# Differential attention: scores from fp32r halves, the next maximum ahead of the subtraction, scores two steps ahead, and local attention in the same order

## The reference

```
s_lat = einsum('bkgqd,bksd->bkgqs', qb, kb) * scale       # |k_pos - q_pos| <= 128
s_ctx = einsum('bkgqd,bkcd->bkgqc', qb, k_ctx) * scale
p = softmax(concatenate([sink_col, s_lat, s_ctx]))
```

```
s = einsum("bqmd,bkmd->bmqk", q_blk * 32 ** -0.5, kf)      # m: 2 maps x 6 heads
p = softmax(s - slopes[:, None, None] * |qpos - kpos|)
a = p[:, :, 0] - lam * p[:, :, 1]
o = einsum("bhqk,bkhe->bqhe", a, vf)
```

## Time and profile before

| | |
|---|---|
| time, median of 3 runs | 4617.31 us (4612.63 to 4624.49) |
| the profiled execution's own time | 4616.67 us |
| its span, first to last instruction | 4614.9 us |
| mean granted TensorE clock | 0.94 |
| TensorE busy (matmul) | 4279.6 us, 93% |
| VectorE, ScalarE, GpSimd busy | 2053.8, 1427.2, 324.4 us |
| differential attention, first layer, first score to last output | 2898.05 to 3025.46 us |
| the same, second layer | 3996.82 to 4126.30 us |
| local attention's steps | about 509 to 653 us |

### The profile page before, as it was taken

How to read it: one execution, slowest core, us unless ns; L and a number is a source line. 1 busy time by engine, 2 the same in 40 slices (tenths; PEclk the granted TensorE clock), 3 DMA queues, 4 the chain that set the end, 5 groups by cost and what they waited for, 6 DMA issues and landing times. The chain is left out here.

```text
span 4614.9 us, 50711 instructions
## 1 busy us (share of the span) xinstructions
PE 4279.6 (93%) x21093; PEld 3224.0 (70%) x21093; DVE 2053.8 (45%) x3082; ACT 1427.2 (31%) x2094; POOL 324.4 (7%) x320
## 2 busy tenths in 40 slices
PE   7899879999999999899999799989998979998998
PEld 2288457788888777578878478457786658546876
DVE  0131566312365333362373564553474455364366
ACT  0121453211253121242361222333462132142254
POOL 0000012000000000000000242000000223100000
PEclk9999888999999999899999899889999989789999
DMA  7611001111112111122222000022222100002231
GB/s 253 236 62 36 9 6 37 55 64 64 56 63 74 55 62 62 38 91 92 97 85 87 6 1 1 5 64 83 91 91 75 40 6 1 5 28 64 91 100 64
DMA packets 254387, 288.69 MB, mean 63 GB/s; under 512 B 6436, under 2 KB 226619, under 8 KB 254197
## 3 DMA queue, kind: packets, MB, share of 16 engines
q1 hardware_dynamic: 254197, 286.04, 18.6%
HBM read 283.92 MB, written 2.10 MB: 62 GB/s over the span
## 5 line engine op out<-in xcount | busy, mean ns | idle before, releaser
L443 PE MATMUL banks<-h_halves,w_halves 128*128 128x512 f32 x3824 | 1426.0, 373 | 84.0 <-DVE h_halves L256 42.4
L444 PE MATMUL banks<-h_halves,w_halves 128*128 128x512 f32 x3824 | 1422.0, 372 | 0.0
L445 PE MATMUL banks<-h_halves,w_halves 128*128 128x512 f32 x3824 | 1414.9, 370 | 0.0
L443 PEld LDWEIGHTS banks<-h_halves,w_halves 128*128 128x128 f32 x3824 | 729.4, 191 | 223.2 <-issue 74.4
L445 PEld LDWEIGHTS banks<-h_halves,w_halves 128*128 128x128 f32 x3824 | 727.1, 190 | 126.0
L444 PEld LDWEIGHTS banks<-h_halves,w_halves 128*128 128x128 f32 x3824 | 729.3, 191 | 119.9
L256 DVE TENSOR_TENSOR w_halves<-work,w_halves 128x2048 fp32r<-128x2048 f32 (+1 forms) x215 | 488.3, 2271 | 549.4 <-ACT w_halves L251 549.3
L251 ACT ACTIVATE w_halves<-work 128x2048 fp32r<-128x2048 f32 (+1 forms) x215 | 407.1, 1894 | 563.2 <-PE banks L445 429.6
L251 ACT ACTIVATE h_halves<-kept 128x512 fp32r<-128x512 f32 (+1 forms) x520 | 332.4, 666 | 314.0 <-PE banks L445 235.2
L256 DVE TENSOR_TENSOR h_halves<-kept,h_halves 128x512 fp32r<-128x512 f32 (+1 forms) x520 | 361.2, 736 | 138.8 <-ACT h_halves L251 138.1
L846 PE MATMUL banks<-work,kept 128*2 128x512 f32 x384 | 170.1, 597 | 10.3 <-DMA work<-in_mod_w 10.3
(11 more groups left out here) (351 smaller groups left out, 4937.2 us busy)
## 6 DMA issues: line engine op xcount, KB each, us to landing
work<-in_w_ff SPq DMA_DIRECT2D x64, 1024.0 KB, 5.1
work<-in_mod_w SPq DMA_DIRECT2D x24, 2048.0 KB, 7.9
work<-in_ffn_w_in SPq DMA_DIRECT2D x44, 1024.0 KB, 5.1
work<-in_odd_w_in SPq DMA_DIRECT2D x24, 1024.0 KB, 5.2
work<-in_w_in SPq DMA_DIRECT2D x24, 1024.0 KB, 4.9
work<-in_ffn_w_out SPq DMA_DIRECT2D x16, 1024.0 KB, 4.9
work<-in_even_w_in SPq DMA_DIRECT2D x13, 1024.0 KB, 5.1
work<-in_odd_w_out SPq DMA_DIRECT2D x8, 1024.0 KB, 4.8
```

Of the source, the lines that this page charges most:

```text
L443: nc.tensor.matmul(o, low[:, k - a, fc], rh[:, tc], start=(k == 0), stop=False)
L444: nc.tensor.matmul(o, high[:, k - a, fc], rl[:, tc], start=False, stop=False)
L445: mm = nc.tensor.matmul(o, high[:, k - a, fc], rh[:, tc], start=False, stop=(k == K - 1))
```

## The change

In differential attention q and k are split into high and low parts, once a stage, three tiles of 128 features each. The scores of a step become the two bias matmuls, then three passes (low q by high k, high q by low k, high by high) of two fp32r matmuls each: the first of a pass is that of map 0 into its bank, the second that of map 1, on the next 32 rows, into the other. The scaling of q moves from GpSimd into the split. The first tile is split ahead of the steps, the second and third in steps 1 and 5. TensorE issues `scores(s+2)` where it issued `scores(s+1)`, and VectorE runs `top(s+1)` ahead of `subtract(s)`. The order of local attention is changed in these two places too, with nothing else in it changed.

```diff
@@ window_stage
             scores(0)
+            scores(1)
             for s in range(N):
-                if s + 1 < N:
-                    scores(s + 1)
+                if s + 2 < N:
+                    scores(s + 2)
                 if s:
                     weigh(s - 1)
                 turn(s)
...
             for s in range(N):
-                normalise(s)
                 if s + 1 < N:
                     top(s + 1)
+                normalise(s)
                 if s:
                     out(s - 1)
@@ diff_stage
+    part = lambda n: core.w_halves[:, n * SEQ:(n + 1) * SEQ]
+    high = [[part(6 * n + t) for t in range(3)] for n in range(2)]
+    low = [[part(6 * n + 3 + t) for t in range(3)] for n in range(2)]
+    tiles_of = lambda n, t: u2(core, 4 + 3 * n + t)
...
+    split_at = {1: 1, 5: 2}
...
         def _(pool):
-            for t in range(3):
-                nc.gpsimd.tensor_scalar(u2(core, 4 + t), u2(core, 4 + t), scale, None, ALU.mult).then_inc(q_scaled, 1)
             pool.wait_ge(loads_in, 80)
-            nc.gpsimd.tensor_copy(dist16, dist).then_inc(q_scaled, 1)
+            nc.gpsimd.tensor_copy(dist16, dist).then_inc(dist_made, 1)
...
                 if s >= 2:
                     pe.wait_ge(exped, 2 * (s - 1))
                 pe.wait_ge(slope_made, h + 1)
+                banks = [core.ps[:, (s % 2) * 2 + m, :] for m in range(2)]
                 for m in range(2):
-                    mp = 2 * h + m
-                    pp = slice((mp % 4) * DD, (mp % 4 + 1) * DD)
-                    bank = core.ps[:, (s % 2) * 2 + m, :]
-                    nc.tensor.matmul(bank, si[h % 2], dist16[:, 3 * P - i * P:3 * P - i * P + SEQ], start=True, stop=False)
-                    mm = nc.tensor.matmul(bank, u2(core, 4 + mp // 4)[pp, i * P:(i + 1) * P],
-                                          u2(core, 7 + mp // 4)[pp, :], start=False, stop=True)
+                    nc.tensor.matmul(banks[m], si[h % 2], dist16[:, 3 * P - i * P:3 * P - i * P + SEQ], start=True,
+                                     stop=False)
+                pe.wait_ge(low_done, 2 * (h // 2) + 2)
+                for n, (q, k) in enumerate(((low[0], high[1]), (high[0], low[1]), (high[0], high[1]))):
+                    for m in range(2):
+                        mp = 2 * h + m
+                        pp = slice((mp % 4) * DD, (mp % 4 + 1) * DD)
+                        mm = nc.tensor.matmul(banks[m], q[mp // 4][pp, i * P:(i + 1) * P], k[mp // 4][pp, :], start=False,
+                                              stop=(n == 2))
                 mm.then_inc(scored, 1)
...
+            def split(t):
+                for n in range(2):
+                    nc.scalar.activation(high[n][t], tiles_of(n, t), ACT.Copy, scale=(scale, 1.0)[n]).then_inc(high_done, 1)
+
+            split(0)
             act.wait_ge(lam_s, 1)
...
             for s in range(N):
                 if s + 1 < N:
                     exps(s + 1)
+                if s in split_at:
+                    split(split_at[s])
                 copy(s)
...
+            def split(t):
+                for n in range(2):
+                    dve.wait_ge(high_done, 2 * t + n + 1)
+                    nc.vector.scalar_tensor_tensor(out=low[n][t], in0=tiles_of(n, t), scalar=(scale, 1.0)[n],
+                                                   in1=high[n][t].bitcast(F32), op0=ALU.mult,
+                                                   op1=ALU.subtract).then_inc(low_done, 1)
+
+            split(0)
             dve.wait_ge(v_turned, 1)
...
             for s in range(N):
-                subtract(s)
                 if s + 1 < N:
                     top(s + 1)
+                subtract(s)
+                if s in split_at:
+                    split(split_at[s])
                 if s:
                     out(s - 1)
```

More of the change, by code:

```diff
@@ L2347, in diff_stage @@
     sc = lambda s, c, w=2: core.sb(GX0 + (s % 2) * 8 + c, w)
+    part = lambda n: core.w_halves[:, n * SEQ:(n + 1) * SEQ]
+    high = [[part(6 * n + t) for t in range(3)] for n in range(2)]
+    low = [[part(6 * n + 3 + t) for t in range(3)] for n in range(2)]
+    tiles_of = lambda n, t: u2(core, 4 + 3 * n + t)
     steps = [(h, i) for h in range(6) for i in range(4)]
     N = len(steps)
-    (loads_in, lam_s, v_turned, v_copied, slope_made, q_scaled, scored, maxed, exped, subtracted, turned,
-     turned_copied, weighted, out_done, chain_s) = core.sems(15)
+    split_at = {1: 1, 5: 2}
+    (loads_in, lam_s, v_turned, v_copied, slope_made, dist_made, high_done, low_done, scored, maxed, exped, subtracted, turned,
+     turned_copied, weighted, out_done, chain_s) = core.sems(17)
     with nc.Block() as block:
@@ L2376, in _ @@
             mm.then_inc(v_turned, 1)
-            pe.wait_ge(q_scaled, 4)
+            pe.wait_ge(dist_made, 1)
             def scores(s):
```

## The result

The changed kernel took 4533.02 us (median of 4 runs, 4532.26 to 4538.15), beside 4616.16 us for the kernel before in the same session (4612.63 to 4624.49). The ratio is 0.9824 [0.9807, 0.984]. The saving is 83 us; 4545 (4520 to 4585) was forecast, a saving of 72. The profiled execution took 4533.55 us, with a span of 4531.8 and a mean granted clock of 0.944.

What follows compares the result with a forecast made beforehand. Differential attention was taken as bound by TensorE at the lower clock level, by a 4.51 us engine ring close to TensorE's 4.25 at the upper; 4616.7 - 31 - 33 - 8 = 4545 us, range 4520 to 4585.

Steps and rivals of the forecast that it cites:

- The ring and the bound: Differential attention, upper level: engine loop of 4.51 us close to TensorE's 4.25; new step 3.35 us, VectorE the bound.
- The pairs run together: Differential attention's scores: each pass's two matmuls overlap, six taking 0.68 us at the upper level and 1.3 at the lower.
- Time at the lower level: Each differential attention stage: 25 us at the lower clock level (1.2 GHz), between an immediate rise and the old 36.
- The first intervals: Start of each differential attention stage: steps of 5.1 us at the lower clock level, TensorE the bound.
- The splits: Splitting q and k in differential attention: 1 us charged a stage; step 5's hidden or up to 1.5 us of VectorE.
- The sum for layer 1, between the maxima: Layer 1's differential attention: 4.4 steps at 5.1 us, 18.6 at 3.35 = 62.3, 1 for splits; whole stage 96 us.
- Local attention: Local attention: the new order removes a wait, saving 8 us of at most 9.4 us of TensorE idle.
- B: Differential attention's score pairs run one after the other, upper step 3.43 us, 107 us a stage: 4565 us; chance 0.15.
- E: The reordering does nothing, upper step stays 4.51 us, local attention gives 0: 4599 us; chance 0.02.
- C: Differential attention: TensorE stands at scores(s+2) while weigh and turn could go, upper step 4.0 us: 4569 us; chance 0.12.
- D: Differential attention: the clock level rises at once, 86 us a stage, savings 41 and 43: 4525 us; chance 0.11.
- A: Clock stays at the lower level through both differential attention stages: 4609 us, or 4673 without pair overlap; chance 0.06.

Runs made afterwards that it cites:

- experiment 1: The changed kernel with the old orders put back in both attentions, so the scores from halves alone: 4591.67 us, ratio 0.9957 to the kernel before.
- experiment 2: The kernel before with both stages' new orders and its f32 scores kept, no splits: 4599.9 us, ratio 0.9965 to the kernel before.
- experiment 4: The changed kernel with both maps' scores multiplied from the same 32 rows, those of map 0: 4568.3 us, ratio 0.9895 to the kernel before.
- experiment 10: The changed kernel with all splits ahead of the steps and differential attention's output copy on ScalarE: 4519.33 us; with two filling matmuls added, 4521.15 us.
- experiment 3: The changed kernel, in differential attention only: maximum behind the subtraction again, 4595.64 us; or instead scores one step ahead again, 4672.14 us.

## Why the prediction was right

The mechanism was right in the steps that carry the saving (two close limits, pairs that run together, VectorE as the new bound), and the size was 11 us short: 6.7 and 4.9 us in the two layers and 2.3 outside the stages, less 2.8 in local attention. Part of the nearness is luck, since terms of both signs were off. By its own steps:

- **The ring and the bound.** Right. "Shortening one alone would stop at the other" is what experiments 1 and 2 measured: 4.51 and 4.24 us a step. VectorE is the new bound; its step is 3.22 or less, not 3.35. Negation and reciprocal now stand together and start 0.08 apart (2957.72, 2957.80), where the 1.46 for maximum and negation had charged 0.20 from the negation's start on.
- **The pairs run together.** Right, and shown by experiment 4, which took the cause away. The size was not 0.68 us for six but 0.89, and at the lower level 1.58, not 1.3. The price of one matmul was right: inside the group the starts are 0.23 and 0.43 us apart, as in the earlier trace rows. What the sum left out are the group's two ends, where TensorE goes from 128 rows to 32 and back: 0.33 and 0.32 instead of 0.23, and 0.59 and 0.56 instead of 0.43. With the same ends six one at a time take 1.58 us, not 1.36, so the rivals without overlap were priced too low as well. The estimate by the Trainium skill's ratio (TensorE: Matmul & The Clock Gate, Part 3) was 0.89 and 1.7 us. The first agrees with the measurement by chance: it charges 0.30 us a pair, and the distance inside the group is 0.23. The extra 0.2 us cost little at the upper level, since TensorE's 2.93 stays at or under VectorE's step.
- **Time at the lower level.** 21.8 and 26.5 us, forecast 25. The number was near by luck, and the shape was not: one stretch of 15 or 16 us, and a second that the split in step 5 brought about and the prediction didn't have.
- **The first intervals.** Charged 5.1 us each; they were 2.5, 3.1 and 5.6. The first two are short since the scores of steps 0 to 2 issue before any weigh or turn; the third has VectorE's wait at `out` in it (experiment 10). Worth 4.1 us a stage.
- **The splits.** Here the cost was larger than forecast. I charged 1 us a stage, at most 1.5 of VectorE. The split in step 1 cost nothing. That in step 5 cost 1.9 (5.1 beside 3.2), and the lower level behind it more: maxima fell by 4.0 and 4.3 us without it.
- **The sum for layer 1, between the maxima.** Forecast 4.4 x 5.1 + 62.3 + 1 = 85.7 us, measured 79.0. The first three intervals gave 4.1 us less, the fourth 1.5 (3.6 for 5.1), the fifth 1.1 (3.0 for 4.05), fifteen upper ones at 3.14 gave 3.2, and the split's interval and the two of the dip behind it (5.1, 5.2, 3.9) took back 3.1: together 6.7, but for rounding.
- **Local attention.** Forecast 8 us, got 5.2. Of the 9.4 us of idle in the earlier trace rows about 1.7 lay in the last steps behind 645 us, which no order fills, and 3.9 stay between 529.2 and 645. All of that is TensorE's weigh waiting for ScalarE's copy (3.9 us, 16 waits); the same wait was 7.2 us in 20 before, from 527 to 645. The stage's start also stayed at the lower level 20.3 us instead of 17.8, which the prediction didn't have; what part of the missing 2.8 us that makes was not separated. TensorE is busy 97% at the upper level, not over 98.

The rivals: B is refuted by experiment 4. E, by which the reordering does nothing, is refuted by experiment 1: without the orders the step stays at 4.51 us and 22 of the 83 us are all that is gained. C is refuted by the gapless VectorE at the upper level; a bite of that kind exists only at the third interval of a stage, at `out`, not at the scores. D did not come. A did not come either, but experiment 3 shows that the lookahead alone separates the changed kernel from it; 0.06 rested on the claim that nothing in the rows spoke for a longer stay at the lower level, and the rows could not tell how near the case was. What sets how long a stage stays at the lower level is not settled by these runs.

## What to carry to other kernels

Where two limits of a step lie close (here 4.51 and 4.25 us), price a change to each with the other one in place, and expect the gain only from both: here 22 and some 15 us from one alone, 83 together. Moving an instruction ahead in a strict queue needs its input one stage earlier too; the maximum ahead of the subtraction without the deeper lookahead made the kernel 56 us slower than the one before, although it had the halves; part of that is TensorE's clock, at its lower level through both stages. And small work inserted in a tight loop (a 1.3 us split) should be priced with the stretch at the lower level that can follow it (here 2 us more than the split's own interval), and be put ahead of the loop where a DMA is being waited for anyway.

## What the runs showed of the hardware

- fp32r matmuls of 32 rows and 512 columns start 0.23 us apart at the upper level and 0.43 at the lower, as those of 128 rows do (0.227 and 0.43). Two on different rows start within 0.02 us of each other and count as one. At the ends of a group, where the rows change from 128 to 32 and back, the distances are 0.33 and 0.32 us, at the lower level 0.59 and 0.56. So three pairs take 0.89 and 1.58 us, six on the same rows 1.58 and 2.86. The pairing came out the same with the maps listed one behind the other.
- A stage in which TensorE idled 1.07 us in each 6.51 us step was granted 0.50 from end to end, over 150 us, twice. With the scores two steps ahead the same instructions were granted 1.00 after 15 and 16 us.
- A wait of 2.10 us in the middle of the upper level was followed by 6.8 to 10.2 us at the lower in eight stages of eight, one of 1.54 us by 3.4 us in one of two. Waits of 0.22 us in many steps were not. The granted clock also fell twice in a stage of the kernel before, for 3.4 and 10.2 us, without a recorded wait of TensorE.
